# A two-layer conformer and attention encoder on one core: 21 of 31 taps on VectorE, sinks on ScalarE, layer norm chain moved up, feed forward ends in PSUM

## What is computed

```python
D_MODEL, SEQ, DEPTH, D_FF = 1024, 512, 2, 2816        # batch 1, float32

for l in range(DEPTH):
    x = x + 0.5 * swiglu(rmsnorm(x, ffn1_norm[l]), ffn1_w_gate[l], ffn1_w_up[l], ffn1_w_down[l])
    u = rmsnorm(x, mix_norm[l]) @ w_in[l]             # 1024 -> 512 a, 512 gate, 512 q, 128 k, 128 v
    y_conv = conformer_conv(u[..., :1024], conv_w[l], conv_b[l], conv_ln_g[l], conv_ln_b[l])
    y_attn = windowed_gqa_sink(q, k, v, attn_sink[l])
    y = concat([rmsnorm(y_conv, out_norm_conv[l]), rmsnorm(y_attn, out_norm_attn[l])])
    x = x + y @ w_out[l]
    x = x + 0.5 * swiglu(rmsnorm(x, ffn2_norm[l]), ffn2_w_gate[l], ffn2_w_up[l], ffn2_w_down[l])
return rmsnorm(x, final_norm)

swiglu(x, g, u, d) = (silu(x @ g) * (x @ u)) @ d
conformer_conv: h = a * sigmoid(gate); h = depthwise convolution of width 31 (+ bias); silu(layernorm(h))
windowed_gqa_sink: 8 query heads, 2 key heads, blocks of 128 queries against the block before, their own and the next;
    scores / 8 - slope * |distance|, masked beyond 128; m = max(scores, sink);
    p = exp(scores - m);  o = (p / (sum p + exp(sink - m))) @ v
```

## Time and profile before

| what | value |
|---|---|
| median of 3 runs | 1883.95 us (1881.65 to 1891.44) |
| profiled execution | 1882.95 us, span 1881.1 us |
| TensorE busy | 1834.1 us, 97% |
| VectorE, ScalarE, GpSimd busy | 984.9, 758.2, 1137.9 us |
| mean granted clock of TensorE | 0.985 of full |
| first mixer: input tiles, attention, output tiles | from 387, 467 and 531 us |
| second mixer: the same | from 1307, 1387 and 1451 us |

### The profile page before, as it was taken

One profiled execution on the slowest core, in us unless ns is written; L12 is line 12 of the kernel. 1 busy time (PEld: TensorE's weight loads), 2 busy tenths in 40 slices (PEclk: granted clock), 3 DMA queues, 4 the chain that ended last, 5 costly groups with the idle time before them and its releaser, 6 DMA issues.

```text
span 1881.1 us, 25283 instructions
## 1 busy us (share of the span) xinstructions
PE 1834.1 (97%) x8160; PEld 1508.1 (80%) x8160; DVE 984.9 (52%) x1203; ACT 758.2 (40%) x988; POOL 1137.9 (60%) x595
## 2 busy tenths in 40 slices
PE   6999999999999999999999999999999999999996
PEld 5888888878778888888878888887877888888885
DVE  7644443369946554443365445334887554454334
ACT  2433332246766333332333433223577644333221
POOL 4544457769667444467744444676885854444774
PEclk9999999999899999999999999999989999999998
DMA  4322223321012322223332232333211122222331
GB/s 146 117 95 100 90 75 100 106 95 62 24 57 92 109 89 100 91 77 94 119 102 90 100 100 74 92 93 112 77 35 46 68 102 99 100 89 81 93 93 58
DMA packets 53425, 166.68 MB, mean 89 GB/s; under 512 B 6000, under 2 KB 6256, under 8 KB 53360
## 3 DMA queue, kind: packets, MB, share of 16 engines
q1 hardware_dynamic: 52128, 163.78, 27.4%
q10 hardware_dynamic: 1232, 2.10, 0.3%
HBM read 163.76 MB, written 2.10 MB: 88 GB/s over the span
## 4 chain that ended last, share of the span: by engine, by line
PE 88%; DVE 5%; issue 4%; POOL 2%; ACT 0%; DVEq 0%; DMA 0%; POOLq 0%; ACTq 0%
PE bank L1150 29%; PE bank L1151 28%; PE bank L1152 28%; DVE xs_hi L848 1%; DVE bank L930 1%; DVE xs_lo L780 1%; PE bank L1274 1%; POOL x L518 1%; PE bank L1261 0%; DVE prob L952 0%; PE bank L1168 0%; POOL w_lo L397 0%; DVE pt_lo L977 0%; DMA x<-xT 0%; PE bank L1263 0%
## 5 line engine op out<-in xcount | busy, mean ns | idle before, releaser
L397 POOL TENSOR_TENSOR w_lo<-stage,w_hi 128x1024 fp32r<-128x1024 f32 x352 | 893.4, 2539 | 639.4 <-ACT w_hi L538 638.9
L538 ACT ACTIVATE w_hi<-stage 128x1024 fp32r<-128x1024 f32 x352 | 373.0, 1061 | 885.6 <-PE bank L1152 882.0
L1150 PE MATMUL bank<-xs_hi,w_hi 128*128 128x512 f32 x1688 | 663.6, 393 | 18.9 <-POOL w_lo L397 11.4
L1152 PE MATMUL bank<-xs_hi,w_lo 128*128 128x512 f32 x1688 | 659.6, 391 | 0.0
L1151 PE MATMUL bank<-xs_lo,w_hi 128*128 128x512 f32 x1688 | 659.5, 391 | 0.0
L1150 PEld LDWEIGHTS bank<-xs_hi,w_hi 128*128 128x128 f32 x1688 | 318.3, 189 | 89.3 <-issue 13.3
L1152 PEld LDWEIGHTS bank<-xs_hi,w_lo 128*128 128x128 f32 x1688 | 318.2, 189 | 66.5
L1151 PEld LDWEIGHTS bank<-xs_lo,w_hi 128*128 128x128 f32 x1688 | 318.3, 189 | 66.2 <-issue 1.4
L807 DVE TENSOR_TENSOR work<-bank,rstd 128x512 f32<-128x512 f32 x176 | 120.6, 690 | 401.2 <-PE bank L1152 400.3
L1152 PE MATMUL bank<-h_hi,w_lo 128*128 128x512 f32 x704 | 274.2, 390 | 0.0
L1151 PE MATMUL bank<-h_lo,w_hi 128*128 128x512 f32 x704 | 274.2, 389 | 0.0
(11 more groups left out here) (152 smaller groups left out, 1411.1 us busy)
## 6 DMA issues: line engine op xcount, KB each, us to landing
stage<-w_gu SPq DMA_DIRECT2D x176, 512.0 KB, 3.3
stage<-w_down SPq DMA_DIRECT2D x64, 384.0 KB, 3.1
stage<-w_down SPq DMA_DIRECT2D x64, 320.0 KB, 2.9
stage<-w_in SPq DMA_DIRECT2D x24, 512.0 KB, 3.3
stage<-w_out SPq DMA_DIRECT2D x16, 512.0 KB, 3.3
x<-xT ACTq DMA_DIRECT2D x4, 512.0 KB, 6.4
stage<-w_in SPq DMA_DIRECT2D x8, 256.0 KB, 2.6
out<-result SPq DMA_DIRECT2D x8, 256.0 KB, 2.2
```

The source lines that it names most:

```text
L397: nc.gpsimd.tensor_tensor(w_lo[:, r, :], stage[:, r, :], w_hi[:, r, :].bitcast(F32), ALU.subtract).then_inc(split, 1)
L538: nc.scalar.activation(w_hi[:, r, :], stage[:, r, :], ACT.Copy).then_inc(hi_made, 1)
L1150: nc.tensor.matmul(to, wh, mh, start=first, stop=False)
L1152: return nc.tensor.matmul(to, wl, mh, start=False, stop=last)
```

## The change

Five things change. VectorE makes 21 instead of 20 of the 31 taps, and more of them stand in the input tiles: 70 instead of 58, with 14 instead of 22 left for attention, from unit 4 to unit 17 (before: two ahead of unit 0, then units 0 to 19). ScalarE and GpSimd make 10 instead of 11 products a channel group, 36 instead of 32 of them before the units. The sinks' exponentials are four instructions of ScalarE for each group, which read the sink and the negated maximum themselves; VectorE's sink_arg is gone. The channel sum, mean, centring and squares of the layer norm stand two to three units sooner, the weight splits of slots 12 to 15 one group sooner, and the variance's matmuls before the last unit. At a feed forward's end the sum stays in its bank of PSUM, from which x, xs_hi, the square and xs_lo are made; the down tiles' banks are given free by xs_lo, and the two loops are unrolled.

```diff
-FFN_TURNS, MIX_TURNS = 2 * NF + ND, 24
+FFN_TURNS, MIX_TURNS = 2 * NF, 24
...
-V_TAPS = 20
+V_TAPS = 21
...
-V_SPREAD = [0, 0, 4, 5, 6, 6, 6, 6, 5, 5, 5, 5, 3, 2]
-P_SPREAD = [0, 0, 2, 3, 3, 3, 3, 3, 3, 3, 3, 2, 2, 2]
-P_LATE = 12
-LATE_TAPS = 20
+V_SPREAD = [0, 0, 5, 6, 7, 7, 7, 7, 6, 6, 6, 6, 4, 3]
+P_SPREAD = [0, 0, 2, 3, 3, 3, 3, 3, 3, 3, 3, 3, 4, 3]
+P_LATE = 4
+FIRST_LATE, LATE_TAPS = 4, 14
...
 # gpsimd, in the loop over groups
+                    if 2 <= g < 6:
+                        mix_low(12 + g - 2)
                     if g == 1:
                         add_channel(1)
                     elif g == 3:
                         add_channel(2)
-                    if g >= 3:
-                        mix_low(12 + g - 3)
...
 # scalar
                 def exp_sink(g):
-                    act.wait_ge(sink_ready, l * N_GROUPS + g + 1)
-                    nc.scalar.activation(sink_exp[:, g % PROBS, :], sink_arg[:, g % PROBS, :], ACT.Exp).then_inc(sink_exped, 1)
+                    for c in range(GROUP):
+                        at = SINK + g % 2 * GROUP + c
+                        nc.scalar.activation(sink_exp[:, g % PROBS, c:c + 1], par[:, at:at + 1], ACT.Exp,
+                                             bias=neg_max[:, g % PROBS, c:c + 1]).then_inc(sink_exped, 1)
...
-                    if 25 <= u < 29:
-                        square_channels(u - 25)
-                    if c == 0 and 3 <= g < 7:
-                        mix_high(12 + g - 3)
+                    if 22 <= u < 26:
+                        square_channels(u - 22)
+                    if c == 0 and 2 <= g < 6:
+                        mix_high(12 + g - 2)
...
 # vector, end of a feed forward
-                with dve.Fori(0, ND // 4) as i:
-                    dve.wait_ge(par_landed, l * 16 + 16)
-                    for j in range(4):
-                        m = i * 4 + j
-                        tile_summed(l, base + 2 * NF + m * 4 + 3)
-                        nc.vector.scalar_tensor_tensor(chunk(x, m), bank[j][:], 0.5, chunk(x, m), ALU.mult,
-                                                       ALU.add).then_inc(evicted, 1)
-                        own(l, turns + 2 * NF + m)
-                        dve.wait_ge(sq_added, prep * ND + m)
-                        nc.vector.tensor_tensor(sq[:], chunk(x, m), chunk(x, m), ALU.mult).then_inc(squared, 1)
-                        high_x(m, par, gain_at)
-                        split_x(prep, m, par, gain_at)
+                dve.wait_ge(par_landed, l * 16 + 16)
+                for m in range(ND):
+                    new_x, no = bank[m % BANKS][:], (2 * l + h_base // NF) * ND + m + 1
+                    tile_summed(l, base + 2 * NF + m * 4 + 3)
+                    nc.vector.scalar_tensor_tensor(new_x, new_x, 0.5, x[:, m, :], ALU.mult,
+                                                   ALU.add).then_inc(x_summed, 1)
+                    dve.wait_ge(x_summed, no)
+                    nc.vector.tensor_copy(x[:, m, :], new_x).then_inc(x_kept, 1)
+                    nc.vector.tensor_scalar(xs_hi[:, m, :], new_x, par[:, gain_at + m:gain_at + m + 1], None,
+                                            ALU.mult).then_inc(x_hi_made, 1)
+                    dve.wait_ge(x_kept, no)
+                    dve.wait_ge(sq_added, prep * ND + m)
+                    nc.vector.tensor_tensor(sq[:], new_x, x[:, m, :], ALU.mult).then_inc(squared, 1)
+                    dve.wait_ge(x_hi_made, prep * ND + m + 1)
+                    nc.vector.scalar_tensor_tensor(xs_lo[:, m, :], new_x, par[:, gain_at + m:gain_at + m + 1],
+                                                   xs_hi[:, m, :].bitcast(F32), ALU.mult,
+                                                   ALU.subtract).then_inc(x_split, 1)
...
 # vector, loop over units (sink_args is gone, and so are its calls and two taps ahead of the loop)
-                        late = int(u < LATE_TAPS)
+                        late = int(FIRST_LATE <= u < FIRST_LATE + LATE_TAPS)
...
-                    if u == LATE_TAPS:
+                    if u == FIRST_LATE + LATE_TAPS:
                         merge(3)
...
-                    if 24 <= u < 28:
-                        centre(u - 24)
+                    if 21 <= u < 25:
+                        centre(u - 21)
...
 # tensor
                 if first == 0:
                     open_bank(l, turn)
+                    if prep is not None:
+                        pe.wait_ge(x_split, prep * ND + BANKS + 1)
...
+                for m in range(ND):
+                    if m < BANKS:
+                        open_bank(l, turns + 2 * NF + m)
+                    else:
+                        pe.wait_ge(x_split, next_prep * ND + m - BANKS + 1)
...
-                    if u == 22:
+                    if u == 20:
                         channel_mean()
-                channel_variance()
+                    if u == 30:
+                        channel_variance()
                 weigh_values(N_GROUPS - 1)
```

59 lines of the change are left out of this document (21 added, 38 removed).

## The result

| | before | after |
|---|---|---|
| median us | 1882.80 (1881.41 to 1891.44, 4 runs) | 1893.97 (1893.49 to 1894.88, 4 runs) |
| ratio to before | | 1.0051, 95% interval [1.0028, 1.0073] |
| profiled span, its clock | 1881.1, 0.985 | 1893.1, 0.984 |

The kernel got slower by half a per cent. The forecast was 1882 us with a range of 1869 to 1890, and a chance of 0.08 for a time above 1893.4.

The account below looks back on a forecast made before the run. TensorE, busy 1834.1 of 1881.1 us, was taken as the bound, losing only idle and low-clock time. Terms -3.2 + 0.9 + 5.2 - 1.6 - 2.2 = -0.9 gave 1882 us, range 1869 to 1890.

Parts of the forecast that it names:

- Part 1: Feed forward ends: xs_hi from PSUM takes 0.7 us, so TensorE's three waits for xs_lo go, -3.2 us.
- Rival C: Feed forward ends: xs_hi from PSUM stays held by GpSimd's w_lo, +2.4, 1884.5 us; chance 0.10.
- the 0.9: Kernel's very end: the later square delays GpSimd's last addition and the stores, +0.9 us, bounds 0.2 and 1.3.
- Parts 2 and 3: Attention head: taps put tile 13's second half +2.2 us later; v_hi comes 4.1 later, unit 4's conversion +2.6.
- and five instead of three before the second: 476: Attention head: GpSimd makes five additions instead of three before the second group's diagonals, which come at 476.
- GpSimd without a gap up to the second diagonals: Sign for part 3, attention head: GpSimd's timeline shows no idle time before the second group's diagonals.
- Part 4: Units 0 to 7: low clock as now, unit 7 late by unit 4's conversion delay of 2.6, +5.2 us for two layers.
- as long as now (10 us): Units 0 to 7: the lower clock was expected again, for the same 10 us as in the kernel before.
- rival B: Attention head: a second low-clock stretch before tile 13's second half, 2.7 to 5 us a layer, 1887.5 to 1892; chance 0.12.
- Part 5: Rest of attention: three VectorE idles go with taps ending at unit 17 and fewer short sums, -1.6 us.
- part 6: Layer norm chain: squares ready before the last unit, factors 1.1 us sooner a layer, -2.2 us.
- rival D: Layer norm chain: factors leave no earlier because of the last unit's conversion on ScalarE, 1884.2 us; within the forecast's 0.46.

Follow-up runs that it names:

- e1: The kernel before with only the feed forward ends in PSUM: 1879.44 us, ratio 0.9983 to before.
- e10: The kernel after with group 4's split behind the channel sum, four products and four taps moved from the input tiles into units 0 to 7: 1888.91 us, ratio 0.9999.
- e12: The kernel after with matmuls whose result nobody reads added in the waits of each attention's head: 1889.91 us, ratio 1.0015 to before.
- e9: e8 with seven unread matmuls a layer added in the attention's head (3, 2 and 2): 1872.53 us, ratio 0.9915 to before.
- e5: The kernel after with one wait more, GpSimd's weight split of group 4 beginning only behind VectorE's last channel sum: 1888.02 us, ratio 1.0014 to before.
- e6: The kernel after with four of ScalarE's and GpSimd's products moved from the last two input tiles to units 0 to 7: 1893.05 us, ratio 1.0040 to before.
- e7: The kernel after with four of VectorE's taps moved from input tiles 8 to 11 to units 0 to 3: 1893.89 us, ratio 1.0044 to before.
- e8: The kernel before with the ends in PSUM, the square ahead of xs_hi there, and weight splits at groups 2 to 5: 1883.95 us, ratio 0.9985 to before.

## Why the prediction was wrong, point by point

- **Part 1, the ends: right.** xs_hi took 0.74 where 0.7 was taken, all three waits went, and e1 alone gives their size. The PSUM rule of the Trainium skill ("VectorE: DVE Perf Modes", "Why PSUM operands drop a tier") has a row now: xs_hi from PSUM runs 0.74 inside w_lo. Rival C is refuted. The end came at +0.8, but the 0.9 was partly luck: in e1 the same block costs 0.3 there, near the forecast's lower bound, and of the other 0.5 in after most is the low clock, at which the last square sums' matmuls (ones, sq_sum) take 1.87 us instead of 1.19.
- **Parts 2 and 3, the lateness of the queues.** With the gain of the first end taken off, the first bias was 2.3 us later (2.6 forecast) and v_hi 4.35 (4.1). Here the sum was right. It failed for GpSimd. The step is "and five instead of three before the second: 476": five additions were put in a row, and "GpSimd without a gap up to the second diagonals" was the sign to look for. GpSimd had a gap of 3.04 us there, since the fourth of them needs a product of ScalarE's (std), which stands behind v_hi, whose lateness the prediction itself had worked out. Before has a gap at the same addition too, 2.31 us ahead of 471.18, of which no row was shown. The diagonals began at 477.69, which is 478.9 without the gain of the first end: 2.9 us later than forecast. Unit 4's conversion, without that gain, was at 480.8 (479.6 forecast).
- **Part 4 was mis-sized by that: +5.2 against +10.0.** The step is "Then unit 7 is late by the 2.6 of part 3", which lets ScalarE's conversion of unit 4 set unit 7. What set it was unit 4 on TensorE, which waits for the diagonals. It comes 24.9 us behind the first score instead of 19.4, and unit 7 follows 9.6 to 9.9 us later at the low clock in both kernels. Without the gain of the first end unit 7 of layer 0 was at 489.5, where 486.6 was forecast: the same 2.9. e10 shows it from the other side: with both queues shorter unit 4 is 3.2 us sooner, and unit 7 3.1 and 2.9.
- **The clock in part 4.** The length "as long as now (10 us)" was no constant even in before, where layer 1 has 13.7 us; in after it was 17 us in layer 0, and in layer 1 3.4 us in tile 13's second half, which is rival B, and 10 more from unit 4 on. But the extra length explains nothing of the miss, as both heads end alike, 34.8 and 34.6 us behind the first score: what was low ahead of unit 4 is hidden by the waits there. Seen from the full clock the loss splits otherwise. e12 and e9 are 3.5 us a layer apart, which are queues; the other 2 of the 5.4 are there because the low clock costs after about 4 us behind unit 4 and before 2 to 2.5.
- **Part 5 failed: -1.6 against +5.8,** and with it the last sentence of part 6, "it ends 5 us before unit 20's mean asks for it". That sentence is about the split of group 3. The one that mattered was that of group 4, which the prediction didn't look at: it lies beside the channel sum, both of whose inputs are in SBUF. The prediction had this lock from the trace, w_lo and xs_hi in the earlier trace rows, and from the Trainium skill ("SBUF — State Buffer", "Who interferes with whom"), and used it for the ends only. e5 shows it: 2.55 us become 0.69, and 6 us of the kernel's time. From unit 15 to unit 23 it takes 14.5 us a layer, after 18.0, before 15.1: the collision costs 3.5 a layer, and without it part 5 is -1.2, near the -1.6 forecast (the first of the three waits, 0.27 at 497.37, lies ahead of unit 15).
- **Part 6: -2.2 against -1.3.** In layer 0 the factors left no earlier, which is rival D's result, though not by its mechanism. From unit 23 to the factors after takes 14.5 us in both layers; before took 14.5 and 15.8. The waits there are 1.23 and 1.01 instead of 0.85, 2.39 and 0.40, about as forecast, but the clock now falls ahead of the factors, as it did before only in layer 1:

```profile
534.00:538.00 4.00, 3.66 (x12) 3.11 (x13) 0.39 (x2) 2.54 (x5) 0.00 (x0) 0.57 0.02 4
```

- **The chances.** Rival B was named and came, and cost nothing in the head. The two losses that count, GpSimd's late diagonals and the collision at the channel sum, were named by no rival. 0.08 was too little, since nobody asked when the input of each GpSimd addition would be there, nor which VectorE instruction each moved GpSimd split would meet.

Open is why the same instructions drop the clock in one execution and not in the next, and why it stays down 17 us here and 41 there. A head without any wait on TensorE was not reached by filling: waits of 0.16 to 0.41 us stay. No run gave GpSimd its product sooner and left the rest of after as it is. So what that one wait costs is read from the traces of after, e6, e7 and e10.

## What to carry to other kernels

When work moves on one engine, write down for each moved instruction that locks a port which instructions of the other engine it now lies beside; one wait more, on the engine that has time, is the cheap cure. When instructions are added to a queue, ask for each when its input arrives, and not only how long it takes: here the late engine was late through another one. When TensorE waits in short pieces, price the clock as well as the waits, and ask where the slower stretch is hidden by a wait behind it; if the waits can't be removed, a few matmuls whose result is dropped may hold it up: three places and seven matmuls a layer took the kernel of e8 from 1883.95 to 1872.53 us, from 0.9985 to 0.9915 of before, each measured on a chip of its own. Split a change into its parts before keeping it: in the traces the ends alone gain, the tables lose, and the sum hides both.
